# First weight fetches issued by SyncE inside the neighbouring computation instead of in blocks of their own

## Time and profile before

| | |
|---|---|
| median of 3 runs | 4969.98 us (4964.69 to 4973.57) |
| the profiled execution's own time | 4970.43 us |
| its span, first to last instruction | 4968.7 us |
| mean granted TensorE clock | 0.882 of full speed |
| PE busy | 3930.5 us (79%) |
| PE's weight loads | 2742.6 us (55%) |
| DVE busy | 2358.3 us (47%) |
| ACT busy | 1612.7 us (32%) |
| POOL busy | 170.8 us (3%) |
| moved by DMA | 905.01 MB, 182 GB/s over the span |

### The profile page before, as it was taken

One profiled execution on the slowest core, in us unless ns is written; L12 is line 12 of the kernel. 1 busy time (PEld: TensorE's weight loads), 2 busy tenths in 40 slices (PEclk: granted clock), 3 DMA queues, 4 the chain that ended last, 5 costly groups with the idle time before them and its releaser, 6 DMA issues. The chain is left out here.

```text
span 4968.7 us, 61247 instructions
## 1 busy us (share of the span) xinstructions
PE 3930.5 (79%) x20597; PEld 2742.6 (55%) x20597; DVE 2358.3 (47%) x4998; ACT 1612.7 (32%) x3031; POOL 170.8 (3%) x148
## 2 busy tenths in 40 slices
PE   5988998885567999999969656999827777777776
PEld 2448995332556788777746545999614532222223
DVE  0435663159875666666626695888353200000001
ACT  1223332110774444444314165666212111111111
POOL 0003431000000000000000000000000000000000
PEclk8979998997888999999989878999966888878788
DMA  7100001141255544445420228999222179999996
GB/s 269 68 0 1 1 1 68 43 177 60 68 168 193 185 177 169 169 173 178 144 96 1 77 68 305 322 318 316 103 102 72 39 313 427 426 427 427 426 427 282
DMA packets 302748, 905.01 MB, mean 182 GB/s; under 512 B 18672, under 2 KB 138736, under 8 KB 277104
## 3 DMA queue, kind: packets, MB, share of 16 engines
q1 hardware_dynamic: 302576, 902.68, 48.1%
HBM read 851.23 MB, written 51.38 MB: 182 GB/s over the span
## 5 line engine op out<-in xcount | busy, mean ns | idle before, releaser
L1630 PE MATMUL pd<-h_parts,u_parts 128*128 128x512 f32 x2048 | 485.7, 396 | 45.5 <-DVE u_parts L1716 45.5
L1643 PE MATMUL po<-act_parts,v_parts 128*128 128x512 f32 x2048 | 482.7, 393 | 10.4 <-DVE v_parts L1721 7.8
L1630 PEld LDWEIGHTS pd<-h_parts,u_parts 128*128 128x128 f32 x2048 | 385.1, 188 | 140.5 <-DVE u_parts L1716 45.7
L2739 PE MATMUL pb<-moe_ring,moe_xs 128*32 128x512 f32 x2048 | 335.9, 760 | 133.7 <-DMA moe_ring<-in_moe_gu 116.8
L1643 PEld LDWEIGHTS po<-act_parts,v_parts 128*128 128x128 f32 x2048 | 383.6, 189 | 104.9 <-DVE v_parts L1721 22.1
L2790 DVE TENSOR_TENSOR moe_hidden<-moe_silu,pg 128x512 f32<-128x512 f32 x16 | 11.0, 688 | 646.5 <-PE pg L2728 480.5
L1836 PE MATMUL pd<-h_parts,u_parts 128*128 128x256 f32 x2048 | 264.1, 283 | 43.1 <-DVE u_parts L1915 43.1
L284 PE MATMUL ps<-hT,w_stream 128*128 128x512 f32 (+1 forms) x672 | 268.9, 563 | 27.8 <-ACTq L304 27.8
L1836 PEld LDWEIGHTS pd<-h_parts,u_parts 128*128 128x128 f32 x2048 | 261.0, 191 | 53.1 <-DVE u_parts L1915 43.3
L1458 PE MATMUL ps<-first_ind,second_ind 128*128 128x128 f32 x1536 | 225.1, 299 | 77.5 <-DVE second_ind L1444 46.3
L2755 PE MATMUL pd<-moe_ring,moe_hidden 128*32 128x512 f32 x1024 | 175.3, 822 | 108.9 <-DMA moe_ring<-in_moe_down 97.8
(11 more groups left out here) (444 smaller groups left out, 6358.4 us busy)
## 6 DMA issues: line engine op xcount, KB each, us to landing
moe_ring<-in_moe_gu SPq DMA_DIRECT2D x128, 2048.0 KB, 26.3
u_stream<-in_peer_u SPq DMA_DIRECT2D x256, 512.0 KB, 6.2
v_stream<-in_peer_v SPq DMA_DIRECT2D x256, 512.0 KB, 4.6
moe_ring<-in_moe_down SPq DMA_DIRECT2D x64, 2048.0 KB, 26.3
ada_ring<-in_ada_w SPq DMA_DIRECT2D x24, 2048.0 KB, 17.6
peer_gates<-gate_stage SPq DMA_DIRECT2D x6, 8192.0 KB, 30.4
g_stream<-peer_gates SPq DMA_DIRECT2D x128, 256.0 KB, 5.0
w_stream<-in_gdn_w_in SPq DMA_DIRECT2D x8, 2048.0 KB, 8.2
```

The lines of the kernel that those rows point to most:

```text
L1630: m = pe.matmul(pd[:, j, 0:T], us[:, j, w, c], h[:, w, c], start=(c + w == 0), stop=(c == DC - 1 and w == 1))
L1643: m = pe.matmul(po[:, (c + b) % 4, 0:T], vs[:, j, w, (c + b) * P:(c + b) * P + P], aparts[:, 4 * half + j, w], start=(j + w == 0), stop=(j ...
L2739: m = pe.matmul(pb[32 * q:32 * q + 32, n % 2, :], xs[:, u % 2, c], w[:, c, :], start=(c < 4), stop=(c >= 4))
```

## The change

`Stream` and `Arrival` no longer open a block when they are made. They get a method `begin(sp)` that issues the same DMAs, and `norm_T`, `modulated`, `normalise_heads`, `rope`, `attend` and `mixer_conv` take a list `begin`; if it isn't empty, their (main) block gets a SyncE part that calls `begin` of each. 23 blocks with SP alone go. One stream, w_v of `memory_layer`, keeps its block through the new method `start`. The order of issue changes in three places: in `gdn_layer` w_qkv goes ahead of w_ab, in `swa_layer` and `mixer_layer` the tables go behind w_q, w_k, w_v and behind w_in. The experts' six tiles move from in front of `pool_mixer` to the block of `mixer_conv`, behind it; w_out of the mixer from in front of two `rms_heads` to `rope`; w_tok and the router's weights to the norm in front. The `wait` blocks stay where they are.

```diff
@@ class Arrival
-        with k.nc.Block() as block:
-            @block.sync
-            def _(sp):
-                for dst, src in pairs:
-                    sp.dma_start(dst, src).then_inc(self.loaded.h, DMA_DONE)
+        self.pairs = pairs
+
+    def begin(self, sp):
+        for dst, src in self.pairs:
+            sp.dma_start(dst, src).then_inc(self.loaded.h, DMA_DONE)
@@ class Stream
+        self.ahead = min(bufs, -(-self.n // BANK))
+
+    def begin(self, sp):
+        for g in range(self.ahead):
+            self.fetch(sp, g, g)
+
+    def start(self, k):
         with k.nc.Block() as block:
             @block.sync
             def _(sp):
-                for g in range(min(bufs, -(-self.n // BANK))):
-                    self.fetch(sp, g, g)
+                self.begin(sp)
@@ norm_T; the same in normalise_heads, rope, attend, mixer_conv
         with nc.Block() as block:
+            if begin:
+                @block.sync
+                def _(sp):
+                    for x in begin:
+                        x.begin(sp)
+
@@ gdn_layer
-                modulated(k, 0, xT, TALL, hT, C("one"), params, mod, "norm1_g", 0)
+                modulated(k, 0, xT, TALL, hT, C("one"), params, mod, "norm1_g", 0, begin=(w_qkv, w_ab))
...
-            normalise_heads(k, oT, 8, TALL, consts, 1.0 / P, lambda h: PARAMS(params, "gdn_norm_g"))
+            normalise_heads(k, oT, 8, TALL, consts, 1.0 / P, lambda h: PARAMS(params, "gdn_norm_g"), (w_z, w_out))
@@ peer_layer
-            modulated(k, layer, xT, T, hT, one, params, mod, "norm2_g", 3, x0)
+            modulated(k, layer, xT, T, hT, one, params, mod, "norm2_g", 3, x0, (w_q, keys))
             keys.wait(k)
@@ swa_layer
-            modulated(k, 1, xT, TALL, hT, CONSTS(consts, "one"), params, mod, "norm1_g", 0)
+            modulated(k, 1, xT, TALL, hT, CONSTS(consts, "one"), params, mod, "norm1_g", 0, begin=(w_q, w_k, w_v, tables))
...
-        rope(k, qT, 8, SEQ, L("swap_a"), L("cos_a"), L("sin_a"))
+        rope(k, qT, 8, SEQ, L("swap_a"), L("cos_a"), L("sin_a"), (w_out,))
@@ mixer_layer
-            norm_T(k, x2, DC, SEQ, hT, C("one"), {(0, SEQ): PARAMS(params, "norm_mix_g")})
             w_tok = Stream(k, c2, W["mix_w_in"][:, 13 * P:13 * P + 400], DC, bufs=1)
+            norm_T(k, x2, DC, SEQ, hT, C("one"), {(0, SEQ): PARAMS(params, "norm_mix_g")}, begin=(w_in, tables, w_tok))
...
-        experts.start(k)
...
-        mixer_conv(k, pT[:, 2:6, :], params)
+        mixer_conv(k, pT[:, 2:6, :], params, (experts,))
...
-        rope(k, aq, 4, SEQ, L("swap_b"), L("cos_b"), L("sin_b"))
+        rope(k, aq, 4, SEQ, L("swap_b"), L("cos_b"), L("sin_b"), (w_out,))
@@ memory_layer
-            norm_T(k, xT[:, :, CTX:TALL], DC, SEQ, hT, C("one"), {(0, SEQ): PARAMS(params, "norm_mem_g")})
+            norm_T(k, xT[:, :, CTX:TALL], DC, SEQ, hT, C("one"), {(0, SEQ): PARAMS(params, "norm_mem_g")}, begin=(w_q, w_k, mem))
...
             w_v = Stream(k, c2, W["ca_wkv"][:, 512:1024], DC, bufs=1)
+            w_v.start(k)
...
-        attend(k, units, SEQ, P ** -0.5, C("ident"))
+        attend(k, units, SEQ, P ** -0.5, C("ident"), (w_out,))
@@ moe_layer, moe_route
+                w_router = Stream(k, c3, W["router_w"], DC, bufs=1)
-                norm_T(k, xT[:, :, CTX:TALL], DC, SEQ, hT, C("one"), {(0, SEQ): PARAMS(params, "norm_ffn_g")})
-                moe_route(k, hT, consts, W, xsT, scatter)
+                norm_T(k, xT[:, :, CTX:TALL], DC, SEQ, hT, C("one"), {(0, SEQ): PARAMS(params, "norm_ffn_g")}, begin=(w_router,))
+                moe_route(k, hT, consts, w_router, xsT, scatter)
...
-        linear_tok(k, hT, DC, 2, logits, Stream(k, ctx, W["router_w"], DC, bufs=1))
+        linear_tok(k, hT, DC, 2, logits, w_router)
@@ class ExpertStream
-    def start(self, k):
-        with k.nc.Block() as block:
-            @block.sync
-            def _(sp):
-                for n in range(W_RING):
-                    self.fetch(sp, 0, n)
+    def begin(self, sp):
+        for n in range(W_RING):
+            self.fetch(sp, 0, n)
```

More of the change, by code:

```diff
@@ L356, in linear_tok, with norm_T @@
     stream.loaded[0].done(DMA_DONE)
-def norm_T(k, xT, kc, T, out, one, mults, adds=None):
+def norm_T(k, xT, kc, T, out, one, mults, adds=None, begin=()):
     nc = k.nc
@@ L552, in gdn_qkv, with normalise_heads @@
     freed.done(24 + 1)
-def normalise_heads(k, vT, heads, T, consts, mean, mult):
+def normalise_heads(k, vT, heads, T, consts, mean, mult, begin=()):
     nc = k.nc
@@ L1185, in residual_linear, with modulated @@
     linear_T(k, hT, kc, T, D, evac, engine="vector", stream=stream)
-def modulated(k, layer, xT, T, out, one, params, mod, gain, part, x0=0):
+def modulated(k, layer, xT, T, out, one, params, mod, gain, part, x0=0, begin=()):
     nc = k.nc
@@ L1202, in modulated @@
         norm_T(k, xT[:, :, x0:x0 + T], DC, T, out, one, {s: mult[:, v] for s, v in spans.items()},
-               {s: shift(v) for s, v in spans.items()})
+               {s: shift(v) for s, v in spans.items()}, begin)
 SUPER = 4
@@ L1994, in peer_layer, with rope @@
             experts_narrow(k, u, v, gates, parts, xT, gain, CONSTS(consts, "ident"))
-def rope(k, vT, chunks, T, swap, cos, sin):
+def rope(k, vT, chunks, T, swap, cos, sin, begin=()):
     nc = k.nc
@@ L2024, in rope, with attend @@
     freed.done(chunks)
-def attend(k, units, nk, scale, ident):
+def attend(k, units, nk, scale, ident, begin=()):
     nc = k.nc
@@ L2443, in mlstm_mixer, with mixer_conv @@
         dve_block(gate_y)
-def mixer_conv(k, qkT, params):
+def mixer_conv(k, qkT, params, begin=()):
     nc = k.nc
@@ L2557, with moe_route @@
 TILES = GU_TILES + DOWN_TILES
-def moe_route(k, hT, consts, W, xsT, scatter):
+def moe_route(k, hT, consts, w_router, xsT, scatter):
     nc = k.nc
```

## The result

The changed kernel takes 4909.69 us (median of 4 runs, 4908.96 to 4912.78) against 4971.02 for the kernel before (median of 4 runs); the ratio is 0.988, with a 95% interval of 0.9863 to 0.9897. The forecast was 4913.0. The profiled execution took 4910.1 us, its span is 4908.3, 60.4 less than the 4968.7 of before. A second measurement of both gave 4908.37 against 4969.46 (ratio 0.9882, 0.9866 to 0.9899).

What follows compares the result with a forecast made beforehand. PE is busy 79% of the span, mostly in untouched expert loops; the change wins where all engines idle behind SP's issuing. 42.2 + 5.7 + 0.8 + 2.2 + 2.4 + 5.0 - 1.3 = 57.0 us less: 4913, range 4900 to 4928.

Steps and rivals of the forecast that it cites:

- SP's issuing, alone on the path: At six places, the time from SP's first issue to the next compute instruction goes: 42.2 us together.
- The small blocks: Four blocks of one or two streams, before the first norm and three attentions' w_out, give 1.4 us each: 5.7.
- w_tok: Its block between norm and projection, issuing one fetch only, goes: 0.8 us.
- the router: Its fetch, issued a norm earlier, has landed when PE starts: 2.2 us gained.
- The boundary's loss: A compute engine leaves a boundary some 0.1 us later than SP, at 13 places: 1.3 us lost.
- PEER layer 1: Behind its norm the wait for the keys becomes visible, so the gain is 2.4 us, not 5.1.
- What was costed at nothing: SP's issuing beside the norms and the landing of first groups, both covered by work running beside them: 0 us.
- Rival 1: Transfers take the stalls' place, first groups landing as late as the keys: 9 us less gain, 4922; chance 0.09.
- The clock: With less idleness PE's clock stays high: 2.6 us in the memory norm, 2.4 in normalise_heads or PEER layer 0; 5.0.
- Rivals 2 and 3: Stall returns within the norm, about 4963, chance 0.04; moved code makes the wide expert loop refetch, 4981, chance 0.03.

Runs made afterwards that it cites:

- Run 1: The changed kernel with each list of first fetches issued in one block of its own in front of the stage, 12 blocks instead of 23: 4975.39 us.
- run 2: The kernel before with only the two gdn_w_out fetches issued inside normalise_heads, w_z keeping its own block: 4963.38 us (one run).
- Run 5: The changed kernel with the keys' fetch issued ahead of the two w_q fetches in peer_layer: 4902.56 us (one run).
- run 6: The changed kernel with AdaParams' first four fetches issued inside the stage that uses them instead of its constructor's block: 4903.85 us (one run).
- runs 4: The changed kernel with 23 blocks at the program's start, each holding only one already satisfied wait of SP: 4915.57 us (one run).
- version 8: The changed kernel with keys fetched ahead of w_q, AdaParams' first fetches inside their stage, and memory's w_v begun in its norm: 4901.46 us, measured again 4895.97.
- four dummies: The changed kernel with keys fetched first and four unread matmuls on PE in the multiplier's block ahead of each modulated norm: 4919.05 us (one run).
- behind one: The changed kernel with keys first, AdaParams' fetches inside, w_v in its norm, and one unread matmul ahead of the 512-token modulated norms: 4900.00 us.

## Why the prediction was right

**SP's issuing, alone on the path** (42.2 us in six places): 41.35. The subtraction of the earlier trace rows was right within 0.06 us in five places of six; the experts' tiles gave 3.35 instead of 4.0. Run 1 brings the whole gain back by nothing but a separate block, run 2 shows that the stall begins with the third fetch: two fetches out of four carry 9.06 of the 10.5 us.

**The small blocks**: 6.2 instead of 5.7, as the block in front of the first norm was worth 2.1 and not the 1.4 of the earlier trace rows; it issues three fetches. w_tok came out as costed, the router at 2.34 instead of 2.2.

**The boundary's loss** (-1.3): not there. I let compute engines leave a boundary 0.1 us behind SP; the rows above show 0.02 to 0.03. This is the one term of the sum that was wrong as a thing, not only in size, and its 1.3 us are a good third of the 3.4 us by which the profiled execution missed the forecast's sum.

**PEER layer 1**: the step that decided most about the method. The naive subtraction gives 5.1 us; I forecast that the wait for the keys becomes visible and leaves 2.4. It left 2.62, and PE leaves the wait 16.4 us behind the first issue, which is my 15.9 to the landing and 0.5 to the projection, where I had 0.6. The multiplier's block ahead of it took 0.5 us and not the 0.7 I had, and these two make up the difference to 2.4. Run 5 takes the wait away by order alone and finds the 4.88 us. The rate was that of the slices of before: in the changed kernel the 5.24 MB go as fast, 21 of the 22 full slices at 375 GB/s or more. By the Trainium skill's rule for the HBM side (DMA: Bandwidth & Descriptors, "Where 436 GB/s comes from"; some 358 GB/s) this place would have given 1.2 us; the measured 2.62 speaks against it.

**What was costed at nothing** stayed at nothing: no projection behind a norm is released by the DMA of its stream, and the norms aren't stretched. Rival 1 needed a late first group and had none. It was right about one place that wasn't in the change: at the program's start (run 6) the transfer does take the block's place, since nothing covers it, and moved behind one more block it made the stage longer.

**The clock** (5.0): 4.89. The memory norm gave 2.57 against 2.6, for the reason given. The rest came out near its term in part by luck. Of `normalise_heads` and PEER layer 0 I counted one without being able to say which; the first profile has it at `normalise_heads` (1.80, and 0.52 at the other), the second at PEER layer 0. In the seven profiles that have both norms as in the changed kernel (it twice, runs 4, 5, 6 and version 8 twice), `normalise_heads` is at the high clock once, PEER layer 0 four times, neither twice (run 5 and version 8's first), always behind 2.74 and 2.45 us of idleness. What I had no term for are later effects of less idleness: behind the first rotation of the window attention the clock is back earlier by 2.3 us in all. Windows of 10 us that begin at the same point of the work, before and after:

```profile
2620.00:2630.00 10.00, 10.00 (x33) 0.56 0.00 0
```

```profile
2585.76:2595.76 10.00, 9.98 (x44) 0.82 0.01 2
```

In the residual linear behind the gated delta net it is 1.7 us less, in the gated delta net itself 1.6 us more, where the change touches nothing. In the memory attention 1.2 us are gained; the start of the program takes 1.3 us more and the stages behind the router 1.1, and how much of these is the clock was not worked out. With smaller ones of either sign they leave 2.2 us.

**Rivals 2 and 3** fell with runs 1, 2 and 4. The instruction queues fetch as much as before on the page, and in the wide expert loop they fetched one packet, as in the earlier trace rows; an offset of all code by 23 blocks moved the wide loops by less than 0.1 us. That more unfavourable places exist was not tried.

## What to carry to other kernels

Ahead of a stage, read two starts: SP's first issue and the next compute instruction; what lies between them is what a separate block of fetches costs, and it is decided by how full the queue is, not by the number of blocks. Before counting it as won, ask what is waited for next and how long the last byte takes from the first issue: where the stage in front is shorter than that, put the fetch that is waited for first at the head of the queue. Where nothing can run beside the transfer, as at the program's start, moving the issue only renames the wait, and a later first issue is paid in full: 2.4 us here. And check an edit place by place: the 9.85 us of run 6 hid that loss.

## What the runs showed of the hardware

A boundary costs 0.39 us with nothing to issue (8.95 us for 23), but about 0.1 us between two fetches into a full queue. Fetches of the same 2 MB differ: the third of a weight stream stalls SP for about 3.6 to 4.6 us, while six of the experts' tiles took 2.94 us together; the sum of bytes alone doesn't set the stall, and what does was not tried. Executions differ in which of two norms runs at the high clock, if any, by 1.7 us each, with the same code and the same idleness in front (2.74 and 2.45 us). With 0.96 us of idleness in front the same matmuls took 7.13 us behind four dummies and 8.58 to 9.89 behind one.
